# Latent attention's groups of four: one set of values between the first score parts, and seven early modulation tiles

## What is computed

```
s = einsum(q, k) * scale;  p = softmax(s);  o = einsum(p, v)
# latent attention: q and k have 64 columns without and 32 with rotary positions
mod = silu(c) @ w_mod + b_mod        # 48 tiles of 128 outputs, for x and ctx
```

## Time and profile before

| | us |
|---|---|
| median of 3 runs (lowest, highest) | 2502.84 (2501.11, 2503.05) |
| the profiled execution | 2505.26 |
| its span | 2503.5 |
| TensorE busy | 2453.6 |
| VectorE busy | 1335.4 |
| ScalarE busy | 548.7 |
| GpSimd busy | 621.4 |

### The profile page before, as it was taken

How to read it: one execution, slowest core, us unless ns; L and a number is a source line. 1 busy time by engine, 2 the same in 40 slices (tenths; PEclk the granted TensorE clock), 3 DMA queues, 4 the chain that set the end, 5 groups by cost and what they waited for, 6 DMA issues and landing times.

```text
span 2503.5 us, 37953 instructions
## 1 busy us (share of the span) xinstructions
PE 2453.6 (98%) x14528; PEld 2024.2 (81%) x14528; DVE 1335.4 (53%) x2707; ACT 548.7 (22%) x1199; POOL 621.4 (25%) x536
## 2 busy tenths in 40 slices
PE   9999999999999999999999999999999999999999
PEld 6757889996799999645567767888888875899999
DVE  6676467741325776324836763545542247435775
ACT  2132122111212221214620002222200215212220
POOL 1101135420212544001012221333241010232543
PEclk9999999999999999999999999999999999999999
DMA  8745344433333453120024662121222120243453
GB/s 313 284 186 201 127 162 153 193 131 135 117 135 119 168 193 135 66 87 26 2 84 156 218 260 88 68 101 71 110 93 80 68 95 26 104 166 153 168 193 110
DMA packets 39128, 334.67 MB, mean 134 GB/s; under 512 B 3920, under 2 KB 9168, under 8 KB 21712
## 3 DMA queue, kind: packets, MB, share of 16 engines
q1 hardware_dynamic: 32080, 307.61, 33.0%
q0 software_dynamic: 6912, 25.17, 2.7%
HBM read 331.72 MB, written 1.05 MB: 133 GB/s over the span
## 4 chain that ended last, share of the span: by engine, by line
PE 89%; DVE 5%; DMA 3%; issue 2%; ACT 1%; POOL 1%; SPq 0%; DVEq 0%; POOLq 0%; ACTq 0%
PE PS L767 25%; PE PS L569 15%; PE PS L1016 11%; PE PS L2799 6%; PE PS L1583 4%; PE PS L1743 4%; PE PS L2840 4%; PE PS L1728 3%; PE PS L2318 2%; PE PS L1384 2%; PE PS L1372 1%; DMA arena<-in_mod 1%; PE PS L436 1%; DMA slot<-in_weights 1%; PE PS L748 1%
## 5 line engine op out<-in xcount | busy, mean ns | idle before, releaser
L569 PE MATMUL PS<-XN,slot 128*128 128x256 f32 (+1 forms) x1184 | 296.8, 411 | 0.8 <-DVE XN L508 0.8
L767 PE MATMUL PS<-SQ,slot 128*128 128x128 f32 (+1 forms) x1984 | 294.4, 301 | 1.8 <-DVE slot L859 1.8
L569 PEld LDWEIGHTS PS<-XN,slot 128*128 128x128 f32 x1184 | 224.4, 190 | 69.8 <-issue 42.5
L767 PEld LDWEIGHTS PS<-SQ,slot 128*128 128x128 f32 x1984 | 268.1, 191 | 14.9 <-DVE slot L859 2.0
L1016 PE MATMUL PS<-arena,slot 128*128 128x128 f32 (+1 forms) x1902 | 251.5, 293 | 3.7 <-DVE arena L1094 2.2
L767 PE MATMUL PS<-XN,slot 128*128 128x128 f32 (+1 forms) x1664 | 250.0, 301 | 0.0
L1016 PEld LDWEIGHTS PS<-arena,slot 128*128 128x128 f32 x1902 | 239.1, 192 | 13.5 <-DVE arena L1094 2.8
L767 PEld LDWEIGHTS PS<-XN,slot 128*128 128x128 f32 x1664 | 226.1, 192 | 10.7
L886 DVE SCALAR_TENSOR_TENSOR arena<-PS,small,arena 128x255 f32<-128x255 f32 (+2 forms) x352 | 174.8, 544 | 44.7 <-ACT arena L830 44.1
L830 ACT ACTIVATE arena<-PS,small 128x256 f32<-128x256 f32 (+1 forms) x176 | 105.3, 617 | 399.3 <-DVE PS L919 238.9
L612 DVE CUSTOM_DVE_ANT_0 arena<-arena 128x1024 f32<-128x1024 f32 x80 | 107.3, 1382 | 30.2 <-DMA arena<-in_mod 30.2
(11 more groups left out here) (302 smaller groups left out, 3828.2 us busy)
## 6 DMA issues: line engine op xcount, KB each, us to landing
slot<-in_weights SPq DMA_DIRECT2D x85, 2048.0 KB, 7.8
slot<-in_weights SPq DMA_DIRECT2D x16, 2816.0 KB, 9.7
slot<-in_weights SPq DMA_DIRECT2D x24, 1536.0 KB, 6.8
arena<-in_mod POOLq DMA_DIRECT2D x48, 512.0 KB, 6.5
arena<-in_mod SPq DMA_DIRECT2D x48, 512.0 KB, 3.3
slot<-in_weights SPq DMA_DIRECT2D x5, 1024.0 KB, 5.5
slot<-in_weights SPq DMA_DIRECT2D x2, 2176.0 KB, 8.4
arena<-in_c SPq DMA_DIRECT2D x2, 1024.0 KB, 12.0
```

The lines of the kernel that those rows point to most:

```text
L569: mm = pe.matmul(o, l, r, start=k == 0, stop=k == len(terms) - 1, skip_group_check=True)
L767: mm = pe.matmul(PS[:, bank, 0:h], lhs[:, k * P:(k + 1) * P], rhs(k), start=first and k == 0, stop=last and k == 3, skip_group_check=True)
```

## The change

In the groups, the values of unit u-4 leave the end of the group before and run between the first parts of unit u and unit u+1 (only in the first piece). In ScalarE's program the output copies move along: a group ends with output(u-4) and output(u-3) in place of output(u-3) and output(u-2), and output(n-4) comes behind copy_t(n-2). Behind the last group values(n-4) keeps its place. Where all units are plain nothing changes. In VectorE's program modulation tile 7 moves from the early tiles to the front of those before `foxin`'s job 2.

```
--- before.py
+++ after.py
@@ -1349,6 +1349,8 @@
             def scores_of_four(u):
                 for p, rope in enumerate(zip(units[u]["rope"], units[u + 1]["rope"])):
                     for v in (u, u + 1):
+                        if p == 0 and v > u:
+                            values(u - 4)
                         for i in range(2):
                             if p == 0:
                                 claim(pe, 2 * (v % 2) + i)
@@ -1399,14 +1401,10 @@
             for u in range(plain, n, 2):
                 scores_of_four(u)
                 turn(u - 2)
-                if u == plain:
-                    values(u - 4)
                 values(u - 3)
                 turn(u - 1)
-                values(u - 2)
-            if plain == n:
-                values(n - 4)
-            else:
+            values(n - 4)
+            if plain < n:
                 late(pe)
             turn(n - 2)
             values(n - 3)
@@ -1461,13 +1459,10 @@
                 exps(u)
                 exps(u + 1)
                 copy_t(u - 1)
-                if u == plain:
-                    output(u - 4)
+                output(u - 4)
                 output(u - 3)
-                output(u - 2)
             copy_t(n - 2)
-            if plain == n:
-                output(n - 4)
+            output(n - 4)
             copy_t(n - 1)
             for u in (n - 3, n - 2, n - 1):
                 output(u)
@@ -2008,7 +2003,7 @@
                     vector=lambda d, mixnorm=mixnorm: vector_norm(d, "mixnorm0", mixnorm),
                     gpsimd=lambda p, mixnorm=mixnorm: gpsimd_norm(p, "mixnorm0", mixnorm))
                 add(vector=lambda d, jobs=jobs: reads_linear(d, VD, "vector", "memkv0", jobs[3:], 3))
-                add(scalar=lambda a: scalar_silu_c(a, 0), vector=lambda d: vector_mod_tiles(d, *range(0, 8)),
+                add(scalar=lambda a: scalar_silu_c(a, 0), vector=lambda d: vector_mod_tiles(d, *range(0, 7)),
                     gpsimd=lambda p: gpsimd_mod_loads(p, range(0, MOD_OUT)))
                 add_tokens("memkv0", lambda k, t: MEMN[0][:, k, t * P:(t + 1) * P], 2, DK, 2, 0,
                            [VM[0][:, 4 * t + 2 * h:4 * t + 2 * h + 2, :] for h in range(2) for t in range(2)])
@@ -2047,7 +2042,7 @@
 
                 def vector_foxin(dve, jobs=fox_jobs):
                     for j, job in enumerate(jobs):
-                        vector_mod_tiles(dve, *{2: range(8, 16), 6: range(16, 23)}.get(j, ()))
+                        vector_mod_tiles(dve, *{2: range(7, 16), 6: range(16, 23)}.get(j, ()))
                         reads_linear(dve, VD, "vector", "foxin", [job], j)
                     vector_mod_tiles(dve, *range(23, 33))
                 add(tensor=lambda pe, jobs=fox_jobs: tensor_linear(pe, "foxin", jobs),
```

## The result

| | before | after |
|---|---|---|
| median of the runs (lowest, highest) | 2502.95 (2501.11, 2507.78), 4 runs | 2523.09 (2518.91, 2528.66), 4 runs |
| the profiled execution, its span | 2505.26, 2503.5 | 2518.91, 2517.1 |
| mean granted clock of the profiled execution | 0.998 | 0.997 |

The ratio is 1.0079, with a 95% interval of 1.0063 to 1.0096: 20 us, against +8 in the prediction, and outside its range. The other three executions of after had mean granted clocks of 0.995, 0.994 and 0.993 and took 2523.53, 2522.65 and 2528.66 us. A thousandth of clock is 2.5 us, so a good part of what lies between them is clock, and the profiled one is the fastest.

What follows compares the result with a forecast made beforehand. TensorE, busy 2453.6 of 2503.5 us, was taken to bound the kernel. Batt0 +4.6, batt1 +2.6, tile 7 -0.9 and a clock fall +1.7 made +8.0, a median of 2510.8 us, range 2505.5 to 2515.0.

Steps and rivals of the forecast that it cites:

- part 1: Batt0 and batt1 groups: moved values opening an output bank wait for ScalarE's later output copy; +4.6 and +2.6 us.
- the middle marks: Starts of the first transposes in middle groups, predicted 7.52 us apart.
- Rival C: Batt0 and batt1: output copy in time, values fill the waits, no stall; -2.8 us with the lambda wait, chance 0.07.
- Rival D: Batt0 and batt1: half of each stall given back, +2.3 and +1.3; total +1.8 us, chance 0.12.
- rival A: Batt0 and batt1: stalls as forecast but no lowered clock; total +6.3 us, chance 0.23.
- part 3: TensorE's clock: one fall behind batt1's 2.96 us stall, costing 1.7 us, and none in batt0.
- Rival B: Lowered clock in batt0 as well, two more falls of 1.7 us; total +11.4 us, chance 0.13.
- part 2: Tile 7, start of forgetting attention: lambda wait of 1.8 us goes, VectorE's late tiles leave -0.9 us.
- term of -0.9: Tile 7's predicted net effect at the start of forgetting attention, in us.
- bound of +0.3: Tile 7's worst case in us: four tiles behind a landing at 151.3.
- Rival E: VectorE in time for forgetting attention, whole lambda wait saved, else as the forecast; total +7.1 us, chance 0.11.

Runs made afterwards that it cites:

- e6: e1 with batt0's three waits filled by repeats of unit u's first score part; 2509.45 us against 2502.53 before.
- e3: e1 with output(u-4) first in each of ScalarE's groups and output(n-4) ahead of copy_t(n-2); 2503.54 us against 2502.68 before.
- e4: The changed kernel with modulation tile 32 made inside forgetting attention, behind VectorE's copies for its fourth unit; 2512.88 us against 2502.68 before.
- e12: The changed kernel with batt0's three waits filled by repeated score parts and tile 32 behind forgetting attention; 2507.80 us against 2501.23 before.
- e1: The kernel before with only the values and output copies moved, tile 7 still among eight early tiles; 2518.27 us against 2502.68 before.
- e10: e3 with tile 32 behind forgetting attention and VectorE's lambda product ahead of the eight early tiles; 2499.05 us against 2502.24 before.
- e11: e5 with batt0's three waits filled by repeats of unit u's first score part; 2503.82 us against 2501.23 before.
- e5: e1 with output(u-4) first in ScalarE's order in the last group of each stage only; 2512.31 us against 2502.53 before.
- e2: The kernel before with only modulation tile 7 moved, groups unchanged; 2508.14 us against 2502.68 before, ratio 1.0014.
- e7: The kernel before with modulation tile 32 made behind forgetting attention; 2501.39 us against 2502.53 before.

## Why the prediction was wrong

**Right: part 1, the output bank.** The mechanism, the places and the size held. There are four waits for the output copy, in groups 16, 20 and 22 and behind batt1, 1.90, 1.47, 1.90 and 2.83, against 2, 1.7, 2.1 and 3 in the prediction; the middle marks are 7.57 to 7.59 apart against 7.52. What they cost without a lowered clock was predicted as +4.6 and +2.6 and is +4.46 and +2.72 (e6). Rival C, that the moved values fill the waits, is out by these four waits; e3, which puts the copy in time, shows what C would have given, 0.5 in batt0 and 0.2 in batt1, where C counts 0.7 and 0.3. Rival D, half given back (+2.3 and +1.3), is out by +4.46 and +2.72, and rival A, stalls with the clock untouched, by the falls below.

**Wrong: part 3, "I take 1.7 ... for one fall in batt1, and none in batt0".** The fall in batt1 came: 1.7 in after, 1.6 in e4 and e12, 2.9 in e1, none in e6. That it fits the 1.7 is in part luck, since that was picked between 1.1 and 2.5. The step that failed is the "none in batt0". The prediction held the gap of 2.79 in the earlier trace rows to be what a lowered clock takes, and 2.96 the only wait in reach, for "the rows show it behind the longest gap only". They did not. The 16 matmuls of 8.12 in the earlier trace rows are a second fall, and the waits just ahead of it were 0.87 and 1.24, among short matmuls (TensorE rows of before, then its window):

```profile
191.14 1.19 PE L436 MATMUL PS<-SQ,small 128*128 128x256 f32 x2 [1.24 <-ACT SQ L446]
```

```profile
192.00:194.00 2.00, 2.00 (x4) 0.88 (x4) 1.86 (x6) 0.02 (x1) 0.00 (x0) 0.50 0.00 0
```

Nor does the gap at L748 settle it: after waits 2.69 there and its 64 matmuls take 8.53 with no fall, e10 waits 2.66 and has one.

In batt0 of after the clock fell to the 1.2 GHz level behind a wait of 1.90 in group 16, between short pieces of work. Filled with matmuls, the same three waits cost 7.3 to 8.8 us less (e6 and e11). Rival B had the direction, at two falls of 1.7, 3.4 in all, and is still less than half of it. The profiled executions show one fall in batt0, worth 1.6, which is less than the medians' 7 to 9. The mean clocks say why for a part of it: after's profiled execution has 0.997 and its others 0.993 to 0.995, e5's 0.999 and four of its others 0.995 to 0.997. Where in those executions the clock fell no trace shows; that it was in batt0 is argued from the filled kernels. The Trainium skill describes the like of it for another kernel, in bf16 ("TensorE: Matmul & The Clock Gate", A second HAM failure mode: psum-queue depth-cycling): a TensorE that idles a little between groups of matmuls, again and again, moves between the two levels. The traces here agree as far as they go, with a fall behind 1.24 and one behind 1.90 in fp32, and the mean clock that rises when the waits are filled.

**Wrong: part 2, "landed at 149.4 to 150.7, and four tiles of 2.29 behind it end at 158.6 to 159.9".** The first half is what e2's profiled execution does: tile 29 is the one that misses the slab, and it lands at 150.53. The step that failed is "four tiles of 2.29 behind it". The fourth, tile 32, has no data then: its load goes out when tile 29 is done, at 153.23, beside the slab at the end of the projection, and takes 9.2 more. The sum had no term for that load or for that slab. The first reduction comes at 164.72.

In after it went one tile further: tile 25, issued at 126.28, took 10.9 to land, tile 28 and not 29 missed the slab of 138.93 (issued at 139.91, 8.0 to land), and tile 32's load met the slab of 152.66 and landed at 162.9. The first reduction came at 165.23, outside the 158.6 to 159.9 that was named as the mark of this step. TensorE's wait is 7.4, and the clock behind it was low as well: forgetting attention is 10.1 longer in the profiled execution, and 2.7 of that is neither the wait nor anything added.

By e2, the term of -0.9 is +5.5 at the median, +3.5 by the ratio: a gain where tile 32 makes it and about +10 more where it doesn't. The bound of +0.3 was wrong for the same reason: it let the landing move by a microsecond, but tile 32's load not wait for tile 29. Rival E is out in the profiled execution, though e2's four runs below 2503 fit what it describes.

**The sum.** Stalls 7.2 (predicted 7.2), the clock behind batt0's stalls some 8 (0), behind batt1's 1.7 (1.7), tile 7 with the lambda wait +5.5 (-0.9): 22, or 20 with e2's ratio, against 20 measured and 8.0 predicted. The miss of 12 is the clock in batt0 and the late tile, in about equal parts. Shown: that each is there (e6, e11; e2, e4) and that without both the changed kernel is at +6.6 (e12), where 7.2, 1.7 and the lambda wait's -1.8 make 7.1. A second count gives the same: after's mean clock of 0.9948 against 0.9986 for before is 9.5 us, and with 7.2 of stalls and 7.4 less 1.8 of waits at the start that makes 22.3; some 2 of it are counted twice, since in the profiled execution about 4.5 us of the low clock lie within the wait of 7.4 itself (162.1 to 166.57), so 20. Open: how much of the gain of the filled waits is something else than clock or chance, and what decides that a tile load takes 7.5 us or 11 beside a slab, on which the race of tile 32 hangs.

## What to carry to other kernels

When a consumer is moved to an earlier place, look for the copy that frees its bank on the other engine and move it ahead of that engine's long work; here this one line decided between 0 and +16 us. Waits of TensorE of about 2 us among short matmuls can cost twice their length: in e5 three of them, 5.3 us in all, cost 9.8 at the median. Look for falls of the clock behind every wait of the kernel before, not the longest alone, and check with matmuls of no use in the gap. For loads in a ring, ask when the last one can be issued, and not only when its turn comes: here it waited for the tile three before it, and then raced a slab. Such a load makes its slot or loses a whole transfer, so take the last of them off the deadline instead of working out its landing to the microsecond.

## What the runs showed of the hardware

The clock's level went down behind a wait of 1.90 us with short fp32 matmuls on both sides (after, window 1230 to 1234, 0.57), but not behind the next ones of 1.47 and 1.90 in the same execution; behind batt1's 2.83 it went down in four of the five profiled executions that have this wait (after, e1, e4, e12, not e6). Such a fall cost 1.6 to 2.9 us. Elsewhere too the same wait lowers the clock in one execution and not in another. In all fourteen profiled executions TensorE waits 1.2 us or more at L436 near 190 us, and in four of them the clock fell there (before, e7, e10, e12). Behind a wait of about 2.7 near 330 us, in two pieces in e2, it fell in eleven, not in after, e5 and e6.

In the profiled executions, from 96 us to forgetting attention, a load of 512 KB issued 0.7 us or more ahead of a slab of 2 MB, and with no other slab beside it, took 3.3 to 3.8 us. One issued between 0.3 us ahead of a slab and 1.1 us behind it took 8.0 to 11.2.
